# Roots of the norms of a two-block transformer kernel: taken on GpSimd as a power of the mean square, in place of a root on ScalarE and an inversion on VectorE

## The reference

```
def rmsnorm(x, g):
    y = x * lax.rsqrt(jnp.mean(x * x, axis=-1, keepdims=True) + EPS)
    return y * g

for i in range(2):                                   # first block
    h = h + hybrid_mixer(rmsnorm(h, norm_mix[i]), ...)    # differential, forgetting and retention heads
    xn = rmsnorm(h, norm_ffn[i])
    h = h + (swiglu(xn, ...) if i == 0 else moe_swiglu(xn, ...))   # dense; then 8 experts, top 2
    gate = sigmoid(rmsnorm(h, ple_norm[i]) @ ple_gate[i])
    h = h + gate * (p[i] @ ple_proj[i])
h = rmsnorm(h, final_norm)
for l in range(2):                                   # second block
    a = rms_norm(h, norm_g[l])
    ...                                              # qa, ka, qm and the keys km of a memory are
    ...                                              # normed per head; so is the output of the hgrn heads
    h = h + (y * silu(z)) @ w_out[l]
```

## Time and profile before

| what | value |
|---|---|
| median of 3 runs | 2052.26 us (2049.85 to 2053.76) |
| the profiled execution: its time, its span | 2050.85 us, 2049.0 us |
| PE, PEld, DVE, ACT, POOL busy | 97%, 82%, 75%, 61%, 0% of the span |
| granted TensorE clock, mean | 0.992 |
| HBM over the span | 245 GB/s |

### The profile page before, as it was taken

One profiled execution on the slowest core, in us unless ns is written; L12 is line 12 of the kernel. 1 busy time (PEld: TensorE's weight loads), 2 busy tenths in 40 slices (PEclk: granted clock), 3 DMA queues, 4 the chain that ended last, 5 costly groups with the idle time before them and its releaser, 6 DMA issues.

```text
span 2049.0 us, 27406 instructions
## 1 busy us (share of the span) xinstructions
PE 1988.4 (97%) x10513; PEld 1679.3 (82%) x10513; DVE 1541.6 (75%) x1513; ACT 1243.8 (61%) x1346; POOL 0.2 (0%) x4
## 2 busy tenths in 40 slices
PE   8999999999899999999999999999998999999998
PEld 7879998887788888888888888888877787878886
DVE  4575556556798988989898888988887746766575
ACT  4554445554677777777777777777776444344532
POOL 0000000000000000000000000000000000000000
PEclk9999999999999999999999999999999999999999
DMA  8617555522799999999999999999975441345320
GB/s 259 220 37 257 186 185 164 166 83 97 256 375 348 355 377 327 374 337 362 369 332 376 335 368 343 354 378 325 374 277 196 164 144 64 122 164 165 123 83 21
DMA packets 243011, 504.07 MB, mean 246 GB/s; under 512 B 12136, under 2 KB 58984, under 8 KB 242920
## 3 DMA queue, kind: packets, MB, share of 16 engines
q1 hardware_dynamic: 242632, 502.71, 68.9%
q10 hardware_dynamic: 288, 0.11, 0.0%
HBM read 501.73 MB, written 1.05 MB: 245 GB/s over the span
## 4 chain that ended last, share of the span: by engine, by line
PE 86%; DVE 7%; ACT 3%; issue 2%; DMA 1%; SPq 1%; DVEq 0%; ACTq 0%
PE bank L694 25%; PE bank L696 25%; PE bank L695 25%; DVE low L1806 2%; PE bank L780 2%; PE bank L806 1%; PE bank L1136 1%; PE bank L1084 1%; PE bank L665 1%; ACT high L1534 1%; ACT high L1328 1%; PE bank L797 1%; PE bank L1236 1%; DMA raw<-in_w_in 1%; PE bank L788 1%
## 5 line engine op out<-in xcount | busy, mean ns | idle before, releaser
L2380 DVE TENSOR_TENSOR low<-raw,high 128x2048 fp32r<-128x2048 f32 x336 | 768.3, 2291 | 105.9 <-ACT high L1534 104.5
L1534 ACT ACTIVATE high<-raw 128x2048 fp32r<-128x2048 f32 x336 | 644.8, 1920 | 247.6 <-PE bank L696 245.9
L1806 DVE TENSOR_TENSOR low<-raw,high 128x2048 fp32r<-128x2048 f32 (+1 forms) x138 | 310.2, 2259 | 162.8 <-ACT high L1328 162.3
L1328 ACT ACTIVATE high<-raw 128x2048 fp32r<-128x2048 f32 (+1 forms) x138 | 260.5, 1893 | 166.5 <-PE bank L696 153.2
L694 PE MATMUL bank<-high,xg_hi 128*128 128x512 f32 x896 | 353.6, 395 | 1.9 <-DVE xg_lo L2363 1.9
L696 PE MATMUL bank<-high,xg_lo 128*128 128x512 f32 x896 | 349.4, 390 | 0.0
L695 PE MATMUL bank<-low,xg_hi 128*128 128x512 f32 x896 | 348.8, 389 | 0.0
L694 PE MATMUL bank<-high,xT_hi 128*128 128x512 f32 (+1 forms) x576 | 227.6, 395 | 7.8 <-DVE low L1806 3.7
L696 PE MATMUL bank<-high,xT_lo 128*128 128x512 f32 (+1 forms) x576 | 221.9, 385 | 0.0
L695 PE MATMUL bank<-low,xT_hi 128*128 128x512 f32 (+1 forms) x576 | 221.7, 385 | 0.0
L694 PE MATMUL bank<-high,hT_hi 128*128 128x512 f32 x536 | 210.1, 392 | 0.0
(11 more groups left out here) (321 smaller groups left out, 2383.7 us busy)
## 6 DMA issues: line engine op xcount, KB each, us to landing
raw<-in_moe_w_gate SPq DMA_DIRECT2D x112, 1024.0 KB, 5.8
raw<-in_moe_w_up SPq DMA_DIRECT2D x112, 1024.0 KB, 6.0
raw<-in_moe_w_down SPq DMA_DIRECT2D x112, 1024.0 KB, 5.9
raw<-in_w_in SPq DMA_DIRECT2D x63, 1024.0 KB, 5.3
raw<-in_w_out SPq DMA_DIRECT2D x20, 1024.0 KB, 4.8
raw<-in_dense_w_gate SPq DMA_DIRECT2D x11, 1024.0 KB, 5.3
raw<-in_dense_w_up SPq DMA_DIRECT2D x11, 1024.0 KB, 5.4
raw<-in_dense_w_down SPq DMA_DIRECT2D x11, 1024.0 KB, 5.0
```

What stands on the lines that cost most here:

```text
L1328: act.activation(high[:, slot, 0:k * n], raw[:, raw_slot[piece], 0:k * n], ACT.Copy).then_inc(high_done, 1)
L1534: act.activation(high[:, k % PARTS, :], raw[:, slot, :], ACT.Copy).then_inc(s["high"], 1)
L1806: dve.tensor_tensor(low[:, slot, 0:k * n], src, high[:, slot, 0:k * n].bitcast(F32), ALU.subtract).then_inc(low_done, 1)
L2380: dve.tensor_tensor(low[:, k % PARTS, :], raw[:, at0 + k % slots, :], high[:, k % PARTS, :].bitcast(F32), ALU.subtract).then_inc(s["low"], 1)
```

## The change

Every root is now one instruction on GpSimd, which raises the mean square to the power -0.5. ACT has no root left, no `sqrt_ahead` and no `serve` for a root; the division by 1024 that the root's scale did is moved into the scale of the squares. DVE asks with a semaphore of its own (`root_asks`), has no reciprocal and no `link` after it, and waits for `root_answers`, or for `xn_ready` where GpSimd writes `rst` itself. In `attention2` the question about `qm` is asked at step 2 as before, but the answer is waited for at step 3. GpSimd answers the 24 questions in a fixed order. A constant tile `minus_half` is set once by DVE.

```diff
         stat = sb("stat", [P, 2, 16])
+        minus_half = sb("minus_half", [P, 16])
...
-            def serve_sqrt(n):
-                serve(stat[:, 1, 0:n], stat[:, 0, 0:n], ACT.Sqrt)
-
             def row_squares(name, t, j):
                 cols = slice(j * CHUNK, (j + 1) * CHUNK)
-                return act.activation(xn[:, t, cols], h[:, t, cols], ACT.Square, accum_out=ssum[:, j, t:t + 1])
-
-            def sqrt_ahead():
-
-                act.activation(marks[:, 62:63], ident[:, 0:1], ACT.Sqrt)
+                return act.activation(xn[:, t, cols], h[:, t, cols], ACT.Square, scale=D ** -0.5,
+                                      accum_out=ssum[:, j, t:t + 1])
...
-            def serve_rstd():
-                serve(stat[:, 1, 0:NT], stat[:, 0, 0:NT], ACT.Sqrt, scale=1.0 / D)
...
+        @block.gpsimd
+        def _(pool):
+            asked = [0]
+
+            def root(n, dst=None, done=root_answers):
+
+                asked[0] += 1
+                pool.wait_ge(root_asks, asked[0])
+                pool.tensor_tensor(stat[:, 1, 0:n] if dst is None else dst, stat[:, 0, 0:n], minus_half[:, 0:n],
+                                   ALU.pow).then_inc(done, 1)
+
+            for l in range(LAYERS):
+                root(NT, rst[:, :], xn_ready)
+                root(8)
+                root(8)
+                root(NT, rst[:, :], xn_ready)
+                root(NT)
+            root(NT)
+            root(NT)
+            for l in range(LAYERS):
+                root(NT)
+                root(8)
+                root(16)
+                root(16)
+                root(8)
+                root(8)
...
+            def root_ask(ins):
+
+                roots[0] += 1
+                ins.then_inc(root_asks, 1)
+
             def rstd_ask(sums, n, scale):
 
-                asked[0] += 1
-                dve.tensor_scalar(stat[:, 0, 0:n], sums, scale, EPS, ALU.mult, ALU.add).then_inc(dve_asks, 1)
-
-            def rstd_answer(n):
-
-                dve.wait_ge(act_answers, asked[0])
-                link(dve.reciprocal(stat[:, 1, 0:n], stat[:, 1, 0:n]))
+                root_ask(dve.tensor_scalar(stat[:, 0, 0:n], sums, scale, EPS, ALU.mult, ALU.add))
 
             def rstd(sums, n, scale):
 
                 rstd_ask(sums, n, scale)
-                rstd_answer(n)
+                dve.wait_ge(root_answers, answers())
+
+            def answers():
+                return roots[0] - shared[0]
+
+            shared = [0]
+
+            def row_ask(name):
+                dve.wait_ge(squares, norm_no[name] + 1)
+                root_ask(dve.scalar_tensor_tensor(out=stat[:, 0, 0:NT], in0=ssum[:, 0, :], scalar=EPS, in1=ssum[:, 1, :],
+                                                  op0=ALU.add, op1=ALU.add))
 
             def rms(name):
 
-                dve.wait_ge(squares, norm_no[name] + 1)
-                ask(dve.scalar_tensor_tensor(out=stat[:, 0, 0:NT], in0=ssum[:, 0, :], scalar=D * EPS, in1=ssum[:, 1, :],
-                                             op0=ALU.add, op1=ALU.add))
-                dve.reciprocal(rst[:, :], stat[:, 1, 0:NT]).then_inc(xn_ready, 1)
+                row_ask(name)
+                shared[0] += 1
                 dve.wait_ge(xn_ready, norm_no[name] + 1)
...
                     if i == 2:
-                        head_squares(qm, 4, P)
+                        squares_of(qm, 4, P)
+                        rstd_ask(rinv[:, 0:8], 8, 1.0 / P)
                     if i == 3:
+                        dve.wait_ge(root_answers, answers())
                         gained(qm, 4, P, g_mem[:, 0, l, :]).then_inc(normed, 1)
...
-            dve.memset(marks[:, 60:61], 0.0).then_inc(table_ahead, 1)
             dve.wait_ge(first_in, FIRST)
+            dve.memset(minus_half[:, :], -0.5)
```

More of the change, by code:

```diff
@@ L240, in program @@
         first_half = sem("first_piece_half_in")
-        early_in, table_ahead = sem("early_consts_in"), sem("table_input_set")
+        early_in = sem("early_consts_in")
         first_high, first_low = sem("first_piece_half_high"), sem("first_piece_half_low")
@@ L247, in program @@
         dve_asks, act_answers = sem("dve_asks"), sem("act_answers")
+        root_asks, root_answers = sem("root_asks"), sem("root_answers")
         setup_dve, squares = sem("setup_dve"), sem("squares_summed")
@@ L1414, in mem_sums @@
                 last.then_inc(mem_squares, 1)
-                serve_sqrt(NT)
             def mem_high(l):
@@ L1580, in finish, with embedding_in @@
                                    scale=slot_gate[:, 0:1]).then_inc(s["y"], 1)
[L1582 to L1586, removed]
+            def embedding_in(l, behind=False):
+                if behind:
                     split_next()
@@ L1611, in _ @@
                 act.dma_start(dst, src).then_inc(first_in, 16)
-            act.wait_ge(table_ahead, 1)
-            act.activation(marks[:, 62:63], marks[:, 60:61], ACT.Sqrt)
             act.wait_ge(first_in, FIRST)
@@ L1627, in _ @@
             half_squares(("mix", 0), 1)
-            serve_rstd()
             split_next()
@@ L1645, in _ @@
                 name = ("ffn", l)
-                sqrt_ahead()
                 norm_high(name, (0, 1))
@@ L1684, in _ @@
                     with act.If(over < 1):
-                        sqrt_ahead()
                         finish(moe_sems[0], moe_first)
-                        embedding_in(1, False)
+                        embedding_in(1, True)
                     for x, n in zip(counts, at_branch):
@@ L1849, in ask @@
                 dve.wait_ge(act_answers, asked[0])
+            roots = [0]
+            def root_ask(ins):
+                roots[0] += 1
+                ins.then_inc(root_asks, 1)
             def rstd_ask(sums, n, scale):
-                asked[0] += 1
-                dve.tensor_scalar(stat[:, 0, 0:n], sums, scale, EPS, ALU.mult, ALU.add).then_inc(dve_asks, 1)
-            def rstd_answer(n):
-                dve.wait_ge(act_answers, asked[0])
-                link(dve.reciprocal(stat[:, 1, 0:n], stat[:, 1, 0:n]))
+                root_ask(dve.tensor_scalar(stat[:, 0, 0:n], sums, scale, EPS, ALU.mult, ALU.add))
             def rstd(sums, n, scale):
                 rstd_ask(sums, n, scale)
-                rstd_answer(n)
+                dve.wait_ge(root_answers, answers())
[6 more added lines that the diff above has]
+                                                  op0=ALU.add, op1=ALU.add))
             def rms(name):
-                dve.wait_ge(squares, norm_no[name] + 1)
-                ask(dve.scalar_tensor_tensor(out=stat[:, 0, 0:NT], in0=ssum[:, 0, :], scalar=D * EPS, in1=ssum[:, 1, :],
-                                             op0=ALU.add, op1=ALU.add))
-                dve.reciprocal(rst[:, :], stat[:, 1, 0:NT]).then_inc(xn_ready, 1)
+                row_ask(name)
+                shared[0] += 1
                 dve.wait_ge(xn_ready, norm_no[name] + 1)
@@ L1899, in norm_rows @@
                 src = norm_input(dve, name)
-                dve.wait_ge(squares, norm_no[name] + 1)
-                ask(dve.scalar_tensor_tensor(out=stat[:, 0, 0:NT], in0=ssum[:, 0, :], scalar=D * EPS, in1=ssum[:, 1, :],
-                                             op0=ALU.add, op1=ALU.add))
-                link(dve.reciprocal(stat[:, 1, 0:NT], stat[:, 1, 0:NT]))
+                row_ask(name)
+                dve.wait_ge(root_answers, answers())
                 if name == "final":
@@ L2026, in attention1 @@
                     if i == 10:
-                        rstd_answer(8)
+                        dve.wait_ge(root_answers, answers())
                         r = stat[:, 1, 0:8].rearrange("p (t h) -> p t h", t=NT)
@@ L2468, in experts @@
                 split_no[0] = moe_first + N_EXPERTS * PER_EXPERT + AHEAD
-                counts = (steps, asked, split_no, high_no, mark_no)
+                counts = (steps, asked, split_no, high_no, mark_no, roots, shared)
                 at_branch = [x[0] for x in counts]
```

15 lines of the change are left out of this document (removed).

## The result

The changed kernel takes 2063.86 us (median of 8 runs, 2059.05 to 2069.26), the kernel before 2053.01 us beside it (8 runs). The ratio is 1.0048, with a 95% interval of 1.0034 to 1.0061: it is slower, by more than the 0.2% that the prediction took as the least that can be told from no change. The profiled execution took 2065.28 us, with a span of 2063.5 us and a mean granted clock of 0.987 where the one before had 0.992.

A forecast was written before the change was run, and what follows sets the result against it. PE, busy 97% of the span, bounds the kernel, so only its waits could move. Terms 0.50 + 0.30 - 0.10 - 0.42 + 1.00 + 0.50 = +1.8 us on the 2052.26 median gave 2054.0 us, range 2050.4 to 2065.2.

The forecast's parts named there:

- The likeliest case: Whole kernel: 2054.0 us, a root on GpSimd taking 0.1 to 1.24 us; own range 2050.4 to 2056.4; chance 0.50.
- slow root: Rival, all roots: GpSimd's power costs well over 1 us, more over 8 and 16 columns; 2065 at 2.13 us; chance 0.29.
- ple: Layer embedding norm: PE waits for its rows; +0.50 us in layer 0, +0.30 in layer 1 after cover of 0.2.
- ffn: Norm in layer 1: without the root, ACT's high parts come 0.34 us earlier; -0.10 us, -0.34 at best.
- final: Final norm: without table load and early root the question comes 0.92 us earlier; later root +0.50, net -0.42 us.
- mix2: Norm of layer 0: with km it delays busy DVE twice, without cover; +1.00 us for both.
- km: Norm in both layers, no cover for PE's low piece: +1.00 us with mix2 in layer 0, +0.50 in layer 1.
- `qa2` and `ka2`: Norms in each layer: DVE delayed twice, 1.00 us against cover of 2.2; nothing, or 1.3 per layer at 2.13 us roots.
- w = 0.9 and d = 0.50: Every root at any width: GpSimd takes w, 0.9 us, and the answer comes d, 0.50 us, later than before.
- ACT gains ... cost at nothing: ACT: 18 of 39 table loads go, some 30 us shorter; no gain for the kernel except where named, as at final.
- A dear first root: Rival, kernel start: the first root alone costs 6 us more, PE stands 4.2 us longer; 2058 us; chance 0.06.
- The cheap root with a faster clock: Rival: roots of 0.10 us, and a gather after 524 running at 2.4 GHz gives 2.3 us; 2048.1 us; chance 0.10.

The follow-up runs named there:

- The wide roots alone: Kernel before, with only the fourteen roots over 8 and 16 columns moved to GpSimd: 2065.27 us beside 2051.88, ratio 1.0064.
- the kernel with the wait filled: Changed kernel, with DVE making the next low halves between asking for the km, qa2 and ka2 roots and taking the answers: 2054.39 us beside 2052.71, ratio 1.0000.

## Why the prediction was partly right

The time lies in the range (2050.4 to 2065.2), near its upper end. The likeliest case, 2054.0 and no measurable change, didn't occur; the *slow root*, which had 0.29, did. The mechanism, a later answer and what covers it at each place, was right, and its main term was mis-sized. That the time fell into the range is partly luck. The upper bound gave every root 2.13 us, and two errors cancel in it: "ple", "ffn", "final" and "mix2", over 2 columns, were to cost 6.9 us and cost about nothing by the sum below, while `km`, `qa2` and `ka2`, over 8 and 16, were to cost 6.0 and cost 8.4.

**The step that failed** is "w = 0.9 and d = 0.50, for every width". The trip is w + 0.28 rather than w + 0.23, and w is 0.70, 1.64 and 2.90 us for 2, 8 and 16 columns, so d is 0.35, 1.29 and 2.56. For two columns the price was good, for sixteen it was a third. The nearest rows, an exponential and a logarithm on ACT, are of an engine that takes 0.40 and 0.42 us over 256 columns (4x256) for the one function and the other; they said nothing of a cost by the column on another engine. The upper bound of 2.13 was too low for 16 columns as well. (A slip beside it: by the prediction's own rows the "ffn" place counts from w = 0.66 and not from 1.0, so its line of 4.1 us lies at w = 1.23 in place of 1.24.)

**Its own sum with the measured sizes.** "ple" layer 0 +0.35, layer 1 +0.15, "ffn" layer 1 -0.25, "final" 0.35 - 0.92 = -0.57, mix2 and `km` of layer 0 0.35 + 1.29 = +1.64, `km` of layer 1 +1.29, and `qa2` and `ka2` 2 x 2.56 less the cover of 2.2, +2.9 in each layer. That is +8.4 us. The start adds 0.9 to 1.4, which makes 9.3 to 9.8, against 9.4 measured at equal clock.

Point by point:
- "ple" of layer 0: PE's wait went from 0.31 to 0.65, +0.34. Right.
- "ple" of layer 1: PE's last product before the rows to their first transposition took 0.23 us, and now 0.38 (1535.44 to 1535.82), +0.15. Right.
- "final": from 1.55 to 0.97, -0.58, where the prediction had -0.42 with a dearer root. Right, and the larger of the change's two gains.
- "ffn" of layer 1: PE's wait there fell from 0.79 to 0.57, -0.22. Right in sign and size.
- `km` has no cover: right, 1.60 us in layer 0 (with "mix2") and 1.01 in layer 1.
- "`qa2` and `ka2`: nothing": wrong, in the way that the prediction gave as a sign of being wrong, a root that grows with the columns. The cover was read rightly, 2.2 us in all; the delay that it had to cover was 5.1 and not 1.0. Measured 2.51 us in each layer.
- By stretches of PE's timeline, layer 0's second attention cost +4.7 us, where the terms make 4.5. Layer 1's cost +2.7 where they make 4.2 and PE's new waits 3.5; before, a low clock in that stretch takes 1.0 us (4 us at 0.74), which the changed kernel's profile hasn't there. The row is of the kernel before:

```profile
1816.00:1820.00 4.00, 4.00 (x14) 3.16 (x14) 2.70 (x2) 0.00 (x0) 0.00 (x0) 0.74 0.96 369
```

- "ACT gains ... cost at nothing": right for what it frees (28.5 us of ACT, worth nothing but at "final"), wrong at one load. The count was right, 39 and 21, but the prediction didn't ask where the next load would go when the first is taken away. That is the term that was missing, 0.9 us by the start of PE's first product and 1.4 by the length of the wait before it.
- A dear first root: it took 0.70 us like the others. The Trainium skill's "GPSIMD Engine Reference", section "Architecture", states some 6 us for the first call of a freshly loaded routine; no such cost shows at this instruction.
- The Trainium skill's "GPSIMD Engine Reference", section "Performance versus the Vector engine", by whose 4497 ns for 2048 columns a column would be some 0.002 us (an estimate), fits the product, 0.0016 us a column, and not the power, 0.157. The prediction said that it prices an addition; it should have given the power a price by the column in a case of its own.
- The cheap root with a faster clock: neither happened; the first gather took 6.58 us (5.88 before), again mostly at the low clock (0.50 from 532 to 536).
- The wide roots alone are 8.7 us at equal clock and their visible waits 7.2. The remaining 1.5 is a little more than the uncertainty of 1.0; where it falls was not followed up.

## What to carry to other kernels

Price an operation by the width that it has at each place, and where no row shows it, let the cost by the column be an unknown of its own. A latency on one engine is paid by whatever is queued behind the wait: asking early and putting other work before the answer gave back 8.7 of 9.4 us with the slow root left in place. When the first use of a table is removed, look where the next load lands; one dummy instruction ahead of the first wait keeps it out of the way.

## What the hardware showed beyond that

- The power on GpSimd takes 0.38 us and 0.157 us a column; the product of the same form 0.20 us, 2 to 16 columns.
- GpSimd's root waits for the rest of a VectorE instruction with two inputs that was there first (2.28 us: +1.98; 1.22 us: +0.91), and for a one-input scaling (0.69 us: +0.38), not for a reduction (1.21 us: 0). In the changed kernel this never shows. VectorE stands still during most of its questions, and where its two-input split begins 0.49 us after the root (for `qm`, 1668.85 after 1668.36) both keep their times, 2.29 and 1.64 us. So it counts which of the two was first. In the kernel with the wait filled the root is slower still, 4.88 us, and the time is that of the kernel before.
- Dips of the granted clock come at the same few places whether the roots are on ACT or on GpSimd, but not in every execution. Most stand behind a wait of PE. Those near 480 us do not: the kernel before has 0.57 from 480 to 484, and PE was busy without a gap from 430. In the comparison of the two profiles of before and after, the clock was worth 5 of 14.5 us.
